# The expert loop of a hybrid decoder step, with the down products moved between the halves of the next expert's gate and up products

## The chip, the cores and the metric

The program runs on one core of a Trainium2 chip. Its time is the device time of one execution in microseconds (us), lower is better; the median of 3 runs of the kernel before is 1805.93 us (1805.49 to 1814.13).

## The reference

One layer of a decoder on 280 tokens (16 meta, 256 prompt, 8 sample tokens), width 2048: norm, a combined input projection, two mixing branches, an output projection; then a mixture of 32 experts, from which each token takes two of one group of eight. Everything is f32. The change touches the experts alone:

```python
p_grp = jax.nn.softmax((xs @ w_coarse + b_coarse).astype(f32), axis=-1)
pg, grp = lax.top_k(p_grp, 1)
...
wt, idx = lax.top_k(jax.nn.softmax(fl_sel, axis=-1), EXPERT_TOP_K)
wt = wt / jnp.sum(wt, axis=-1, keepdims=True) * pg
gate = jnp.zeros((n, N_EXPERTS), f32).at[jnp.arange(n)[:, None], eidx].add(wt)
hg = jnp.einsum('nd,edf->nef', xs, w_gate)
hu = jnp.einsum('nd,edf->nef', xs, w_up)
act = jax.nn.silu(hg) * hu * gate.astype(x.dtype)[:, :, None]
out = jnp.einsum('nef,efd->nd', act, w_down)
```

Per expert w_gate and w_up are 2048 x 512 and w_down is 512 x 2048: three times 4 MiB, 12.58 MB; over 32 experts 402.7 MB.

## The kernel before

The first 740 us or so hold everything ahead of the experts. The routing then makes, on chip, for each expert a rank of its tokens. An expert works on at most 64 tokens (CAP) in a round; further rounds exist for longer lists and are not entered in this input.

**The ring.** All weights pass through `ring`, six slots of 2 MiB. An expert's gate and up weights are cut in two halves along the contracted dimension: the first half sits in slots 2 and 3, the second in 0 and 1 (`MOE_SLOT`). Its down weights are cut in two as well, slots 4 and 5. Each of these six transfers is issued by SyncE (SP), by `load_gate_up` and `load_down`, and waits until PE has used up the slot (`gate_up_done`, `down_done`). Expert 0's six transfers are issued before the loop, while the output projection still runs. In this text a *piece* is a pair of such transfers: first half of gate and up, second half of gate and up, or down.

**An expert x on each engine**, in the kernel before:

- PE (`round_pe`): the list of expert x+1 (`list_of`, 3 small matmuls), gate and up products of x, first and second half (line 1279, 16 matmuls each, which the trace counts as 32), the 16 transposes of the token rows of x+1 (`transpose_rows`, line 1246), the 4 turns of the hidden rows of x (also line 1246), the down products (line 1300, again 16, counted as 32).
- DVE (`round_dve`): the one-hot places for a later list (line 1778), the indices (lines 1783 to 1788), the product h = silu(gate) * up * weight (line 1820), the copy of the turned h (1825), the token rows of x+1 with the gain (1793).
- ACT (`round_act`, unchanged): silu and the copy of up (719, 720), then the four copies of the down results (725).
- GpSimd (`round_rows`): the indirect DMA that scatters the rows of x to `expert_rows` (848), then the gather of the token rows of x+2 (827). These two run on a DMA queue of their own. A gather or scatter has 64 places; places beyond the tokens of the expert are skipped by the bounds check.

PE therefore has, in order, gate/up(x) first half, gate/up(x) second half, down(x), and SP issues loads in the same order, each piece one expert ahead. After the last expert the rows of `expert_rows` are read back, added to x1, normed and stored.

## Time and profile before

| | us |
|---|---|
| median of 3 runs | 1805.93 |
| lowest, highest | 1805.49, 1814.13 |
| the profiled execution | 1807.39 |
| its span, first to last instruction | 1805.5 |
| stage of the experts' loads, first refill issued to last landing | 748.5 to 1747 |

| busy share | PE | PEld | DVE | ACT | POOL |
|---|---|---|---|---|---|
| of the span | 82% | 47% | 33% | 15% | 17% |

The times in the rows below count from the span's start. PE is TensorE's matmuls and PEld its weight loads, DVE VectorE, ACT ScalarE, POOL GpSimd. The share of the DMA engines is a mean over 16 of them. A DMA's time to landing runs from its issue until the last of these engines has delivered its part.

### The profile page before, as it was taken

To read this page: it belongs to the slowest core of one execution; us is meant where nothing else is said; L and a number is where in the kernel's file an instruction comes from. 1 tells how busy PE (TensorE), PEld (TensorE's weight loads), DVE (VectorE), ACT (ScalarE), POOL (GpSimd) and SP (SyncE) were. 2 spreads that over 40 slices of the span, in tenths; PEclk is the share of its full clock that TensorE was granted. 3 is DMA by queue.
4 is the path that set the end of the run, shared out by engine and by line. 5 is a ranking of instruction groups with operands and counts; after the bars stand their busy time and mean duration, and the time that the engine had idled before them with its cause. 6 is when DMAs were issued, how large, how long until landed. Compare 5 with 4: busy or idle time off the path is not lost.

```text
span 1805.5 us, 19311 instructions
## 1 busy us (share of the span) xinstructions
PE 1483.1 (82%) x7485; PEld 853.9 (47%) x7485; DVE 601.2 (33%) x1475; ACT 272.0 (15%) x501; POOL 308.2 (17%) x426
## 2 busy tenths in 40 slices
PE   6999898879988998798878878878877888787780
PEld 6776666567766776443333323323332333233330
DVE  2789999966654113201010100101001010010015
ACT  1100001143331001011111111111111111011111
POOL 0055555443310110000000000000000000000006
PEclk9999899999998999799889889898998989898885
DMA  9433322344513644599999999999999999999954
GB/s 268 141 96 127 105 80 95 107 137 123 171 48 79 221 187 168 215 425 427 420 410 391 408 386 403 418 397 401 396 406 394 405 401 395 397 391 399 393 211 154
DMA packets 130319, 505.28 MB, mean 280 GB/s; under 512 B 23716, under 2 KB 99700, under 8 KB 102780
## 3 DMA queue, kind: packets, MB, share of 16 engines
q1 hardware_dynamic: 112908, 493.74, 70.7%
q0 software_dynamic: 5200, 9.19, 1.6%
q10 hardware_dynamic: 12160, 1.67, 0.7%
q8 instruction: 32, 0.52, 0.1%
q14 instruction: 19, 0.16, 0.0%
HBM read 503.19 MB, written 26.28 MB: 293 GB/s over the span
## 4 chain that ended last, share of the span: by engine, by line
DMA 32%; PE 23%; POOL 2%; issue 1%; DVE 1%; ACT 1%; SPq 1%; POOLq 0%; ACTq 0%; DVEq 0%
DMA ring<-in_w_up_dram 31%; PE bank L1279 17%; PE bank L1300 4%; DVE arena L1820 1%; SPq L383 1%; PE bank L1246 0%; POOL arena L872 0%; POOL arena L871 0%; POOL arena L879 0%; ACT arena L720 0%; POOL arena L880 0%; ACT arena L719 0%; DMA ring<-expert_rows 0%; DVE arena L1825 0%; DMA arena<-x_rows,idx_tok 0%
## 5 line engine op out<-in xcount | busy, mean ns | idle before, releaser
L1279 PE MATMUL bank<-ring,arena 128*64 128x512 f32 x2048 | 486.0, 630 | 97.8 <-DMA ring<-in_w_up_dram 97.8
L1279 PEld LDWEIGHTS bank<-ring,arena 128*64 128x64 f32 x2048 | 196.7, 145 | 360.0 <-issue 359.9
L1300 PE MATMUL bank<-ring,arena 128*64 128x512 f32 x1024 | 277.4, 704 | 18.9 <-DVE arena L1825 18.9
L1820 DVE SCALAR_TENSOR_TENSOR arena<-arena,gcol 64x512 f32<-64x512 f32 x32 | 35.8, 1118 | 635.6 <-ACT arena L720 635.6
L948 PE MATMUL bank<-arena,ring 128*128 128x280 f32 x768 | 195.2, 415 | 0.4 <-DVE arena L1352 0.4
L848 POOL DMA_INDIRECT expert_rows<-arena,idx_dst x32 | 29.4, 920 | 952.1 <-ACT arena L725 952.1
L1300 PEld LDWEIGHTS bank<-ring,arena 128*64 128x64 f32 x1024 | 84.3, 161 | 188.6 <-issue 188.6
L948 PEld LDWEIGHTS bank<-arena,ring 128*128 128x128 f32 x768 | 150.2, 198 | 44.1 <-issue 7.6
L725 ACT ACTIVATE arena<-bank 64x512 f32<-64x512 f32 x128 | 75.7, 592 | 366.7 <-PE bank L1300 365.6
L1246 PE MATMUL bank<-ident,arena 64*128 64x64 f32 x721 | 67.9, 245 | 73.8 <-DVE arena L1820 50.3
L1209 PE MATMUL bank<-ring,arena 128*128 128x256 f32 x512 | 114.6, 386 | 0.0
L1246 PEld LDWEIGHTS bank<-ident,arena 64*128 64x128 f32 x721 | 59.3, 161 | 104.1 <-DVE arena L1820 53.9
L1209 PEld LDWEIGHTS bank<-ring,arena 128*128 128x128 f32 x512 | 98.1, 193 | 16.9 <-issue 3.7
L1783 DVE TENSOR_SCALAR idx_tok<-bank 64x1 uint32<-64x1 f32 x33 | 5.0, 150 | 238.2 <-PE bank L1239 238.2
L1029 PE MATMUL bank<-arena,ring 128*128 128x280 f32 x256 | 75.3, 422 | 0.0
L719 ACT ACT_TABLE_LOAD x16 | 20.5, 1283 | 307.7 <-PE bank L1279 307.7
L940 PE MATMUL bank<-ring,arena 128*128 128x256 f32 x256 | 60.5, 395 | 0.0
L775 POOL TENSOR_TENSOR arena<-arena 128x272 f32<-128x272 f32 x32 | 24.9, 777 | 198.5 <-DVE arena L1538 110.1
L719 ACT ACTIVATE arena<-bank,rcol 64x512 f32<-64x512 f32 x32 | 21.8, 683 | 226.0 <-PE bank L1279 225.8
L940 PEld LDWEIGHTS bank<-ring,arena 128*128 128x128 f32 x256 | 49.9, 198 | 11.0 <-issue 4.2
L1530 DVE TENSOR_TENSOR_SCAN arena<-sc,arena 128x272 f32<-128x272 f32 x64 | 50.0, 820 | 1.1
L1029 PEld LDWEIGHTS bank<-arena,ring 128*128 128x128 f32 x256 | 45.1, 194 | 9.3 <-issue 1.3
(337 smaller groups left out, 1423.9 us busy)
## 6 DMA issues: line engine op xcount, KB each, us to landing
ring<-in_w_down_dram SPq DMA_DIRECT2D x64, 2048.0 KB, 21.2
ring<-in_w_gate_dram SPq DMA_DIRECT2D x64, 2048.0 KB, 18.2
ring<-in_w_up_dram SPq DMA_DIRECT2D x64, 2048.0 KB, 22.9
ring<-in_w_in_dram SPq DMA_DIRECT2D x20, 2048.0 KB, 8.2
ring<-in_w_out_dram SPq DMA_DIRECT2D x8, 2048.0 KB, 9.4
ring<-in_s_w_glu_dram SPq DMA_DIRECT2D x2, 2048.0 KB, 8.4
arena<-v_samples SPq DMA_DIRECT2D x8, 512.0 KB, 4.6
ring<-expert_rows SPq DMA_DIRECT2D x4, 1024.0 KB, 10.2
```

The lines of the kernel that those rows point to most:

```text
L719: nc.scalar.activation(sg[0:CAP, :], PB[b][0:CAP, :], ACT.Silu, scale=rcol[b][:, 0:1])
L725: ins = nc.scalar.activation(yout[b][0:CAP, cc * 512:(cc + 1) * 512], PB[2 + cc // 2][(cc % 2) * CAP:(cc % 2 + 1) * CAP, :], ACT.Copy)
L848: pool.indirect_dma_start(out=y_dram, out_offset=bass.IndirectOffsetOnAxis(ap=idx_dst[b][:, 0:1], axis=0), in_=yout[b][0:CAP, :], in_offse ...
L940: ins = pe.matmul(bank[:, tile * CB:(tile + 1) * CB], xnT[:, k, tile * P:(tile + 1) * P], w[:, k, :], start=(k == 0), stop=(k == KD - 1))
L948: ins = pe.matmul(bank[:, 0:T], w[:, k, b * P:(b + 1) * P], xnT[:, k, :], start=(k == 0), stop=(k == KD - 1))
L1029: ins = pe.matmul(PB[2][:, 0:T], slot(s, KD)[:, k, (i % 2) * P:(i % 2 + 1) * P], xnT[:, k, :], start=(k == 0), stop=(k == KD - 1))
L1209: ins = pe.matmul(PB[unit % 4][:, tile * CB:(tile + 1) * CB], yT[k][:, tile * P:(tile + 1) * P], slot(s, KD)[:, k, :], start=(k == 0), sto ...
L1246: return pe.matmul(out, rows, eye, start=True, stop=True) if waits else pe.transpose(out, rows, eye)
L1279: ins = pe.matmul(PB[b][at:at + CAP, :], xgT[b][:, kk, :], slot(s, KD // 2)[:, k, :], start=(kk == 0), stop=(kk == KD - 1))
L1300: ins = pe.matmul(PB[2 + cc // 2][at:at + CAP, :], hT[:, f, :], slot(4 + half, KF // 2)[:, k, cc * 512:(cc + 1) * 512], start=(f == 0), st ...
L1530: step.add(nc.vector.tensor_tensor_scan(Gs[:, z], sc5[:, 0, j:j + 1].broadcast_to([P, TP]), Wt[:, z], 0.0, ALU.mult, ALU.add))
L1820: STT(hk, sk, gcol[b][:, 0:1], uk, ALU.mult, ALU.mult).then_inc(h_made, 1)
```

## The change

PE's order becomes: list of x+2, gate/up(x) second half, gate/up(x+1) first half, turns of h(x), token rows of x+2, down(x). So silu and the product for x happen while PE has the first half of the next expert, and lists, gathers and transposed rows are made two experts ahead. SP's order follows: gate/up(e+1) first half, down(e), gate/up(e+1) second half. The list's small result has two places in bank 7 now, since its destination and weight columns are read later. GpSimd issues the gather of x+3 first and the scatter of x behind it. The extra, empty list behind the last expert is no longer made: 32 gathers instead of 33.

On PE, one expert in the loop. Of the kernel before (line 1239 the list, 1279 gate and up, 1246 transposes, 1300 down):

```order
463 L1239 MATMUL bank<-route,arena 64x4
464 L1274 ISA
465 L1279 MATMUL bank<-ring,arena 64x512 x16
466 L1274 REGISTER_ALU
467 L1279 MATMUL bank<-ring,arena 64x512 x16
468 L1285 ISA
469 L1246 MATMUL bank<-ident,arena 128x64 x16
470 L1287 REGISTER_ALU
471 L1246 MATMUL bank<-ident,arena 128x64 x4
472 L1292 REGISTER_ALU
473 L1295 REGISTER_ALU
474 L1300 MATMUL bank<-ring,arena 64x512 x16
```

Both halves of one expert stand together, then the 16 token transposes, the 4 turns of h and the down products. The same place in the changed kernel (1250 the list, 1273 gate and up, 1257 transposes, 1292 down):

```order
457 L1250 MATMUL bank<-route,arena 64x4
458 L1268 ISA
459 L1273 MATMUL bank<-ring,arena 64x512 x16
460 L1266 REGISTER_ALU
461 L1268 ISA
462 L1273 MATMUL bank<-ring,arena 64x512 x16
463 L1257 MATMUL bank<-ident,arena 128x64 x4
464 L1310 ISA
465 L1257 MATMUL bank<-ident,arena 128x64 x16
466 L1287 REGISTER_ALU
467 L1292 MATMUL bank<-ring,arena 64x512 x16
```

What moved: the second group at line 1273 belongs to the next expert, and the turns of h stand behind it and ahead of the 16 token transposes.

On SP, the loads of one expert in the loop, with the semaphore that each waits for. Before:

```order
76 L383 ISA [waits gate_up_done]
77 L383 DMA ring<-in_w_gate_dram 128x4096
78 L383 DMA ring<-in_w_up_dram 128x4096 [waits gate_up_done]
79 L383 ISA [waits gate_up_done]
80 L383 DMA ring<-in_w_gate_dram 128x4096
81 L383 DMA ring<-in_w_up_dram 128x4096 [waits gate_up_done]
82 L389 DMA ring<-in_w_down_dram 128x4096 [waits down_done] x2
```

In the changed kernel, in the loop over e:

```order
80 L383 ISA [waits gate_up_done]
81 L383 DMA ring<-in_w_gate_dram 128x4096
82 L383 DMA ring<-in_w_up_dram 128x4096 [waits gate_up_done]
83 L494 ISA
84 L389 ISA [waits down_done]
85 L389 DMA ring<-in_w_down_dram 128x4096
86 L389 ISA [waits down_done]
87 L389 DMA ring<-in_w_down_dram 128x4096
88 L383 ISA [waits gate_up_done]
89 L383 DMA ring<-in_w_gate_dram 128x4096
90 L383 DMA ring<-in_w_up_dram 128x4096 [waits gate_up_done]
```

The two down transfers stand between the two halves of the next expert; the number and size of transfers are the same.

```diff
@@ SP
             def round_loads(R):
-                with sp.Fori(1 if is_first(R) else 0, NE) as e:
+                def gate_up_half(e, half):
                     x = e + R * NE
-                    for q in range(4):
-                        sp.wait_ge(gate_up_done, x * 2 + (q // 2 - 1))
+                    for q in (2 * half, 2 * half + 1):
+                        sp.wait_ge(gate_up_done, x * 2 + (half - 1))
                         load_gate_up(e, q)
...
+                gate_up_half(1, 0)
...
+                gate_up_half(1, 1)
+                with sp.Fori(1, NE - 1) as e:
+                    gate_up_half(e + 1, 0)
+                    down(e)
+                    gate_up_half(e + 1, 1)
+                down(NE - 1)
@@ GpSimd
+            def rows_of_pair(R, i, gathers):
                 for b in range(2):
                     x = i * 2 + (R * NE + b)
-                    g = i * 2 + (R * (NE + 1) + b + 1)
-                    pool.wait_ge(tr_done, g)
-                    gather(g, 1 - b)
...
+                    if b < gathers:
+                        pool.wait_ge(tr_done, x + 3)
+                        gather(x + 3, 1 - b)
                     pool.wait_ge(rows_ready, x + 2)
...
+                    pool.wait_ge(scattered[b], i * 16 + (R * (NE // 2) + 1) * 16)
+                    pool.sem_inc(rows_free, 1)
@@ PE
+            def pair_pe(R, i, last):
+                for b in range(2):
+                    x = i * 2 + (R * NE + b)
+                    if not last:
+                        pe.wait_ge(dst_ready, x + 1)
+                        list_of(x + 2, i * 2 + (b + 2), b)
+                    gate_up(x, b, 1)
+                    if not (last and b):
+                        gate_up(x + 1, 1 - b, 0)
+                    turn_h(x)
+                    if not last:
+                        pe.wait_ge(gathered[b], i * 16 + (R * (NE // 2) + 2) * 16)
+                        transpose_rows(b)
+                    down(x)
...
+                for e in range(2):
+                    list_of(R * NE + e, e, e)
...
+                transpose_rows(0)
+                gate_up(R * NE, 0, 0)
...
+                transpose_rows(1)
@@ DVE
+            def pair_dve(R, i, lists, turns):
+                for b in range(2):
+                    x = i * 2 + (R * NE + b)
+                    if turns:
+                        tokens(x + 2, b)
+                    dve.wait_ge(act_ready, x + 1)
...
+                    STT(hk, sk, gcol[b][:, 0:1], uk, ALU.mult, ALU.mult).then_inc(h_made, 1)
+                    dve.wait_ge(hT_done, x + 1)
...
+                    if turns:
+                        columns(b)
+                        rows_in(x + 2, b)
+                    if turns or b == 0:
+                        destinations(x + 1, 1 - b)
+                    if b < lists:
+                        places(i * 2 + (b + 3))
```

## Rows read from the trace of the kernel before

**Rows 1.** The page's 40 slices of the span, 45 us each

```profile
PE   6999898879988998798878878878877888787780
...
PEclk9999899999998999799889889898998989898885
DMA  9433322344513644599999999999999999999954
GB/s 268 141 96 127 105 80 95 107 137 123 171 48 79 221 187 168 215 425 427 420 410 391 408 386 403 418 397 401 396 406 394 405 401 395 397 391 399 393 211 154
```

**Rows 2.** Groups by line, 748.5 to 1747: xcount, busy us, mean ns, idle before

```profile
L1279 PE MATMUL bank<-ring,arena 128*64 128x512 f32 x2016 | 477.3, 628 | 97.8 <-DMA ring<-in_w_up_dram 97.8
L1300 PE MATMUL bank<-ring,arena 128*64 128x512 f32 x992 | 267.4, 701 | 18.3 <-DVE arena L1825 18.3
...
L1246 PE MATMUL bank<-ident,arena 64*128 64x64 f32 x704 | 65.6, 243 | 69.3 <-DVE arena L1820 50.3 <-DMA arena<-x_rows,idx_tok 19.0
```

**Rows 3.** Windows, whole stage: length, busy us by engine, PEclk, DMA share, GB/s

```profile
748.50:1747.00 998.50, 812.99 (x3898) 344.09 (x3894) 105.20 (x282) 134.72 (x204) 57.54 (x62) 0.90 0.98 400
```

**Rows 4.** Chain that ended last, 1200 to 1300: start us, us, what

```profile
1192.46 28.39 DMA ring<-in_w_up_dram
...
1220.98 8.71 PE bank L1279 x32
...
1230.27 19.84 DMA ring<-in_w_up_dram
...
1250.24 7.10 PE bank L1279 x32
...
1257.92 26.70 DMA ring<-in_w_up_dram
...
1294.58 19.85 DMA ring<-in_w_up_dram
```

**Rows 5.** DMA issues between 1215.7 and 1216.5: count, KB, us to landing

```profile
ring<-in_w_gate_dram SPq DMA_DIRECT2D x1, 2048.0 KB, 19.9
ring<-in_w_up_dram SPq DMA_DIRECT2D x1, 2048.0 KB, 24.4
```

**Rows 6.** Windows, 1220 to 1235

```profile
1220.00:1225.00 5.00, 4.02 (x12) 1.43 (x14) 0.00 (x0) 0.00 (x0) 0.00 (x0) 0.57 1.00 426
...
1227.50:1230.00 2.50, 2.50 (x16) 0.87 (x12) 0.00 (x0) 0.21 (x1) 0.00 (x0) 1.00 0.52 223
1230.00:1232.50 2.50, 1.19 (x18) 1.05 (x17) 1.18 (x2) 1.07 (x2) 0.00 (x0) 1.00 0.86 288
```

**Rows 7.** Line 383, gate and up loads, issued 756 to 1740

```profile
DMA to landing us min/median/max: 10.5/19.9/28.4
```

**Rows 8.** Line 389, down loads, issued 756 to 1740

```profile
DMA to landing us min/median/max: 11.0/21.4/26.4
```

**Rows 9.** Line 383, two loads issued one at a time, 670 to 700

```profile
DMA to landing us min/median/max: 7.2/7.3/7.3
```

**Rows 10.** Last load of the stage, issued between 1727 and 1729

```profile
ring<-in_w_down_dram SPq DMA_DIRECT2D x1, 2048.0 KB, 19.3
```

**Rows 11.** Timeline, first experts: start us, us, engine, line, idle before

```profile
730.32 0.15 DVE L1783 TENSOR_SCALAR idx_tok<-bank 64x1 uint32<-64x1 f32 x1 [0.96 <-PE bank L1239]
...
731.54 1.15 POOL L827 DMA_INDIRECT arena<-x_rows,idx_tok  x1 [17.42 <-DVE gcol L1785]
...
737.09 1.29 DVE L1793 TENSOR_TENSOR arena<-bank,gain_ffn 128x512 f32<-128x512 f32 x2 [6.42 <-PE bank L1246]
...
739.32 1.11 PE L1279 MATMUL bank<-ring,arena 128*64 128x512 f32 x1
...
748.46 0.35 SPq L383 DMA_DIRECT2D ring<-in_w_gate_dram  x1
```

**Rows 12.** Timeline, end of an expert's down products, 1242 to 1247

```profile
1242.32 2.40 ACT L725 ACTIVATE arena<-bank 64x512 f32<-64x512 f32 x4 [11.24 <-PE bank L1300]
...
1242.60 0.15 DVE L1783 TENSOR_SCALAR idx_tok<-bank 64x1 uint32<-64x1 f32 x1 [7.78 <-PE bank L1239]
...
1245.54 0.92 POOL L848 DMA_INDIRECT expert_rows<-arena,idx_dst  x1 [34.39 <-ACT arena L725]
...
1246.77 0.94 POOL L827 DMA_INDIRECT arena<-x_rows,idx_tok  x1 [0.30 <-issue]
```

**Rows 13.** Timeline, last expert

```profile
1724.23 3.77 SPq L389 DMA_DIRECT2D ring<-in_w_down_dram  x2
...
1736.46 7.09 PE L1279 MATMUL bank<-ring,arena 128*64 128x512 f32 x32 [1.63 <-DMA ring<-in_w_up_dram]
...
1747.49 9.97 PE L1300 MATMUL bank<-ring,arena 128*64 128x512 f32 x32 [0.59 <-DVE arena L1825]
```

More of the change, by code:

```diff
@@ L1251, in transpose_rows, with gate_up @@
                 ins.then_inc(tr_done, 1)
+            def gate_up(x, b, half):
+                if half == 0:
+                    pe.wait_ge(xgT_ready, x + 1)
+                sg_, su_ = MOE_SLOT[2 * half], MOE_SLOT[2 * half + 1]
+                pe.wait_ge(slot_loaded[sg_], x * 16 + 16 * (FILLS[sg_] + 1))
+                pe.wait_ge(slot_loaded[su_], x * 16 + 16 * (FILLS[su_] + 1))
+                for k in range(KD // 2):
+                    kk = half * (KD // 2) + k
+                    for at, s in ((0, sg_), (CAP, su_)):
+                        ins = pe.matmul(PB[b][at:at + CAP, :], xgT[b][:, kk, :], slot(s, KD // 2)[:, k, :],
+                                        start=(kk == 0), stop=(kk == KD - 1))
+                ins.then_inc(gate_up_done, 1)
@@ new lines, in turn_h, with down @@
+            def turn_h(x):
+                pe.wait_ge(h_made, x + 2)
+                for f in range(KF):
+                    ins = turn_64(PB[6][:, f * CAP:(f + 1) * CAP], hh[0:CAP, f * P:(f + 1) * P], f == 0)
+                ins.then_inc(hT_done, 1)
+            def down(x):
+                pe.wait_ge(hT_ready, x + 1)
+                pe.wait_ge(rows_ready, x + 1)
+                for half in range(2):
+                    pe.wait_ge(slot_loaded[4 + half], x * 16 + 16)
+                    for k in range(KF // 2):
+                        f = half * (KF // 2) + k
+                        for cc in range(4):
+                            at = (cc % 2) * CAP
+                            ins = pe.matmul(PB[2 + cc // 2][at:at + CAP, :], hT[:, f, :],
+                                            slot(4 + half, KF // 2)[:, k, cc * 512:(cc + 1) * 512],
+                                            start=(f == 0), stop=(f == KF - 1))
+                    ins.then_inc(down_done, 1)
@@ L1305, in _ @@
+                pair_pe(R, NE // 2 - 1, True)
             run_rounds(pe, round_pe)
@@ L1828, in _ @@
+                destinations(x0, 0)
+                for e in range(2):
+                    rows_in(x0 + e, e)
+                with dve.Fori(0, NE // 2 - 2) as i:
+                    pair_dve(R, i, 2, True)
+                pair_dve(R, NE // 2 - 2, 1, True)
+                pair_dve(R, NE // 2 - 1, 0, False)
             run_rounds(dve, round_dve)
```

127 lines of the change are left out of this document (40 added, 87 removed).

## The prediction

> **What bounds the kernel now.** I read the 40 slices first. From slice 18 to slice 38 the DMA row stands at 9 and the rate at about 400 GB/s, while PE drops to 7 and 8 [rows 1]. That is the expert stage, and only it is touched. Then I read the groups by line in it: PE waits 97.8 us for the up weights, 50.3 for the product h, 18.3 for the copy of the turned h, 19.0 for gathered rows [rows 2]. PE is busy 813 of 998.5 us, the DMA engines 0.98 [rows 3]. So the stage looks bound by loads, but not quite full, and the question that decides is whether the missing 2% is something a new order can get back.
>
> The chain answers it. Four second-half up loads, one per expert, land at 1192.46 + 28.39 = 1220.85, then 1250.11, 1284.62 and 1314.43 [rows 4]. Six transfers of 2 MiB land in each gap: 29.26, 34.51 and 29.81 us. The shortest gap is 4.88 us a transfer, 12.58 MB in 29.26 us or 430 GB/s, which is the rate of a full window too (426) [rows 6]. So in that gap the engine that lands last never paused. Yet inside the same gap, from 1227.5 to 1232.5, the mean share falls to 0.52 and 0.86 and the rate to 223 and 288 GB/s [rows 6]. Both hold at once only if the 16 engines aren't level: at 1227.5 the loads issued at 1215.4 and 1215.8 are still 8 and 12.7 us from landing (19.9 and 24.4 us after issue [rows 5]), so some engine has two or more transfers ahead of it while about half have nothing. A load counts as landed when the last engine has it. The dips are idle time of the early engines. The late one sets the pace.
>
> Is the late one ever empty? A load that meets no other takes 7.2 us [rows 9]: 4.88 of transfer and 2.3 of start. In the stage none took under 10.5 us, and the median is 19.9 and 21.4 [rows 7, 8]. Every load was thus issued at least 3.2 us, mostly some 12 us, before the late engine could begin it. Freeing a slot earlier lengthens that queue and brings nothing forward.
>
> The stage adds up on that reading. First refill issued at 748.46 [rows 11]; last load issued at 1727.7 (second of the pair that starts at 1724.23 [rows 13]), landing 19.3 us later [rows 10], at 1747.0: 998.5 us. It has 31 x 6 = 186 transfers: 7.3 for the first, 185 x 4.88 = 902.8, and 88.4 left. In each expert there is one scatter and one gather, so a pair of them costs the late engine 88.4 / 31 = 2.85 us. (The chain agrees: the 34.51 us gap is 5.2 longer than 29.26 and takes in two pairs.)
>
> At this place a rule of the Trainium skill speaks against the change. DMA: Bandwidth & Descriptors, section Latency and other measured facts, says that DMA engines 7 and 15 are usually slower, by its best guess since descriptors of GpSimd's transfers are fetched through their ports. The trace agrees as far as it can: some engines fall behind here, but which ones they are, and whether they are always the same, no row tells. By that rule the gain is nil, as in the sum below.
>
> **The change part by part.**
>
> *Silu and h behind the next expert's first half.* PE's waits for h and its copy, 50.3 + 18.3 us [rows 2], go, and so should most of the 19.0 for gathered rows. PE's own work stays (477.3 + 267.4 + 65.6 us, about 26 of 32.2 us an expert). What is late next is the same thing as now, the late engine: PE reaches each piece earlier and waits there. Worth 0 in the sum. If this cover were gone, i.e. if PE set the pace, the 69 us would be the gain.
>
> *The order of the loads.* Same 186 transfers, same slots; each is again issued when PE has used up the piece three pieces back. A piece is used up at most 9.97 us after it lands (slow case of 32 matmuls [rows 13]), and at that time two pieces, 4 x 4.88 = 19.5 us, are still to come. 19.5 - 10.0 - 2.3 = 7.2 us in hand. Cost 0.
>
> *Gather ahead of scatter.* Now the scatter is issued at 1245.54 and the gather at 1246.77 [rows 12]. In the new order the gather waits for the indices alone, 1.2 us after they start (730.32 to 731.54 [rows 11]), so at about 1243.8; the scatter still waits for ACT's copies, which end at 1244.7, so about 1245.5. They stand 1.7 us apart rather than 1.2, in the other order, with the same 64 places each. Both queue behind the same weight traffic. I take the price of a pair as unchanged. Its bounds: from 0 (-88 us over the stage) to, with nothing shared between the two any more, twice 2.85 (+88); the row nearest to it is today's pair, so the middle, and I keep half a microsecond a pair either way, 15 us, in mind for the range. POOL's queue has a longer wait in it: the gather of x+3 behind the landing of the scatter before. That one was issued an expert, 32 us, earlier. Nothing is held up.
>
> *One gather fewer.* The empty one behind the last expert goes. It moves no rows; between 0 and 2.85 us, I take -0.4.
>
> *The start.* The list of expert 1 comes before the rows of expert 0 are there, so the first product can start when DVE's gain ends at 737.09 + 1.29 = 738.4 instead of 739.32 [rows 11]: -0.8. Behind the first half PE now does 16 transposes and a list before the second (1.8 us), and then the first half of expert 1 before its next refill is issued. By durations of the rows: first piece refilled at 747.6, landing at 754.9 and 759.8; second half done and refilled at about 757, landing by 769.5; first half of expert 1 from 759.8, 7.1 to 8.7 us, so its refill goes out at 767 to 768.6 and its data can flow 2.3 later, 769.3 to 770.9. The queue could run dry for 0 to 1.4 us, once. I take +0.5.
>
> *The end.* Last lands down(31), as now; before it the second half of expert 31, as now at 1736.3. But PE has then been idle since down(30), which landed two transfers earlier (1726.5) and takes some 4.4 us more: about 5 us idle instead of 1.63. After an idle of 5.77 us PE's clock is granted at 0.57 on average over 5 us (1.2 GHz for most of it [rows 6]) and 32 matmuls take 8.71 us instead of 7.10 [rows 4]: +1.6, in the path, since the down products of the last expert follow. Bounds 0 to 2.9 (7.10 to 9.97).
>
> Sum: 1807.39 - 0.4 - 0.8 + 0.5 + 1.6 = 1808.3 for a profiled execution. The profiled one stood 1.46 above its median of 1805.93, so 1806.8 for the median.
>
> **The rivals.**
>
> *The dips are refilled (faster).* If the late engine isn't a fixed few, or its lag comes from late refills, then earlier and more even refills give the idle share back. For it: the rate falls under 400 GB/s in slice after slice [rows 1], and the rate in them is half. Trace Analysis, section Optimization Strategy, of the Trainium skill says that consistent bubbles can mean too little room for the next tile, which would here be slots freed late; this trace has the bubbles, but the loads behind them were already issued. Against it: the shortest landing of 10.5 us, and 29.26 us for six transfers right across a dip. Gain: by share 2% of 998.5, 20 us; by rate 998.5 x (1 - 400/428) = 65 us, which takes in the pairs' real cost. Middle 42: 1765 us.
>
> *The indirect pair gets dearer (slower).* One mechanism: gather and scatter, 1.2 us apart now, share what they cost the late engine; issued in the other order and further apart, they pay more apiece. It decides from 0.3 us a pair on (31 x 0.3 = 9 us). For it: pairs cost 2.85 us though they move few bytes, so the price is one of handling, not of volume. Against it: both still lie in the air together. At +0.8 us a pair 25 us: 1832 us.
>
> *The change doesn't do what it says:* PE's wait for h stays since PE reaches the turns before ACT and DVE are through. They need about 4 us, the half in between 7.1. And the time would be the same.
>
> **How the numbers follow.** No change that matters 0.70 (its own range 1799 to 1815: start and end, and a fifth of a microsecond a pair); dips refilled 0.17 (1742 to 1787); dearer pairs 0.13 (1817 to 1850). 0.5% is 9 us, about what can be told from no change here. Faster: 0.17 + 0.04 of the first case's edge = 0.21. Slower: 0.13 + 0.05 = 0.18. Same: 0.61. Range 1780 to 1824: it leaves out about 0.13 below and 0.07 above.
>
> **What would show it.** Right: the last load lands about 998 us after the first refill; no line's shortest landing comes under about 9 us past the start; six transfers between two second-half up loads still take 29.3 us or more; PE's waits for line 1820's successor are gone and its waits for ring loads have grown by about as much, now on down weights too. The dips stay, perhaps smaller. Wrong: a stage under 980 us with the rate above 410 GB/s (dips refilled), or over 1010 us with loads landing as slowly as now (dearer pairs), or landings near 7.2 us in mid-stage (the queue runs dry).

## The result, and the profile after

The changed kernel takes 1794.98 us (median of 5 runs, 1794.28 to 1797.34), the kernel before 1808.01 (5 runs, 1805.49 to 1814.13): ratio 0.993, 95% interval 0.991 to 0.9949. That is 0.7% faster. The forecast was 1806.8 us and no change. The time lies in the range of 1780 to 1824 that was given, but below the 1799 to 1815 of the case that had 0.70 of the chances.

The profiled execution took 1796.58 us, 10.8 less than before. Its page, in the same 40 slices as [rows 1]:

```profile
PE   6999889879988999697878778788877878878770
...
PEclk9999999889998999698989999898998899889985
DMA  9423323334522753599999999999999999999944
GB/s 270 141 94 99 122 84 97 115 102 126 173 81 62 219 208 137 217 392 424 422 418 403 404 419 402 386 418 405 407 402 407 400 408 413 408 407 403 414 198 155
```

The picture is the old one: 9 in the DMA row from slice 18 on, and PE at 7 and 8. Only the rate is a little higher, 404 GB/s over the stage instead of 400. PE's groups by line in the stage (count, busy us, mean ns, idle before and its releaser) are to be compared with [rows 2]:

```profile
L1273 PE MATMUL bank<-ring,arena 128*64 128x512 f32 x2016 | 522.5, 678 | 183.3 <-DMA ring<-in_w_up_dram 183.3
L1292 PE MATMUL bank<-ring,arena 128*64 128x512 f32 x992 | 219.7, 596 | 0.5 <-DVE arena L1838 0.5
L1257 PE MATMUL bank<-ident,arena 64*128 64x64 f32 x682 | 55.3, 234 | 0.0
```

The waits for h, its copy and the gathered rows, 50.3 + 18.3 + 19.0 us, are gone but for 0.5 us. The one wait left to speak of is for the up weights: 183.3 us instead of 97.8, or 85.5 more for the 87.6 that went. That exchange bought nothing. The whole stage, from first refill to last landing, is to be compared with [rows 3]; the last two columns are DMA share and GB/s:

```profile
747.10:1733.90 986.80, 801.53 (x3870) 319.63 (x3870) 105.32 (x274) 134.70 (x204) 56.52 (x61) 0.91 0.99 404
```

986.8 us instead of 998.5 carries the gain: the stage starts 1.3 us earlier (747.12 for 748.46), is 11.7 shorter, and what follows its last landing is 2.2 longer (60.7 for 58.5): -10.8 in all.

The chain of waits, four landings of second-half up loads as in [rows 4] (start, us):

```profile
1194.57 22.43 DMA ring<-in_w_up_dram
...
1227.80 20.77 DMA ring<-in_w_up_dram
...
1258.94 21.85 DMA ring<-in_w_up_dram
...
1290.32 21.55 DMA ring<-in_w_up_dram
```

They land at 1217.00, 1248.57, 1280.79 and 1311.87: gaps of 31.57, 32.22 and 31.08 us, none under 29.3. From 771 us on no gate or up load took under 11.9 us to land and no down load under 13.3, so each was still issued well before the last engine could begin it. What lies in each gap beside six transfers is GpSimd's pair, here from the timeline (start, us), against [rows 12]:

```profile
1246.22 0.93 POOL L843 DMA_INDIRECT arena<-x_rows,idx_tok  x1 [28.65 <-DVE idx_tok L1810]
1248.22 0.92 POOL L857 DMA_INDIRECT expert_rows<-arena,idx_dst  x1 [1.07 <-ACT arena L741]
```

The gather now stands 2.0 us ahead of the scatter, where it stood 1.2 us behind it. For the transfers issued between 760 and 1730 us, issue to landing takes this long, first the gathers, then the scatters:

```profile
DMA to landing us min/median/max: 7.9/9.0/11.0
...
DMA to landing us min/median/max: 8.2/10.1/12.1
```

The same of the kernel before, gathers and scatters:

```profile
DMA to landing us min/median/max: 10.1/11.6/14.1
...
DMA to landing us min/median/max: 7.6/8.6/10.7
```

In both kernels the one that stands behind takes longer to land, but the pair as a whole shrank: 1.2 + 11.6 = 12.8 us from first issue to last landing, now 2.0 + 10.1 = 12.1.

By the prediction's own formula, (stage - 7.3 - 902.8) / 31, a pair cost the late engine 2.85 us before and 2.47 now. 2.6 us of the new stage are a dry queue at the start (below), and without them it is 2.39. By this reckoning 31 x 0.46 = 14.3 us is what the pairs gave back, and 14.3 - 2.6 = 11.7. It closes by construction, since the pairs get all that is left over; whether it is they that changed is for the runs to show.

### The profile page after: what moved, and what is told of

Same layout as the page of the kernel before. It is cut to its first block, busy times and chain, and to the rows that moved or that the text cites. A ratio compares the mean times of both kernels' runs of the same rounds, so it can differ in the third digit from the quotient of the medians.

```text
span 1794.6 us, 19292 instructions
## 1 busy us (share of the span) xinstructions
PE 1472.8 (82%) x7462; PEld 828.1 (46%) x7462; DVE 602.2 (34%) x1468; ACT 271.9 (15%) x501; POOL 305.8 (17%) x425
## 4 chain that ended last, share of the span: by engine, by line
DMA 40%; PE 25%; DVE 1%; POOL 1%; issue 1%; SPq 1%; ACT 0%; POOLq 0%; ACTq 0%; DVEq 0%
DMA ring<-in_w_up_dram 39%; PE bank L1273 15%; PE bank L1220 6%; PE bank L1292 1%; PE bank L929 1%; SPq L383 1%; DMA ring<-expert_rows 0%; PE bank L1187 0%; PE bank L1170 0%; POOL arena L890 0%; PE bank L1198 0%; POOL arena L891 0%; PE bank L1257 0%; PE bank L1240 0%; DVE arena L1877 0%
## 5 line engine op out<-in xcount | busy, mean ns | idle before, releaser
L1273 PE MATMUL bank<-ring,arena 128*64 128x512 f32 x2048 | 531.4, 678 | 184.7 <-DMA ring<-in_w_up_dram 183.3
L1273 PEld LDWEIGHTS bank<-ring,arena 128*64 128x64 f32 x2048 | 188.2, 155 | 503.2 <-issue 501.6
L843 POOL DMA_INDIRECT arena<-x_rows,idx_tok x32 | 30.1, 942 | 862.3 <-DVE idx_tok L1810 862.0
L1292 PEld LDWEIGHTS bank<-ring,arena 128*64 128x64 f32 x1024 | 71.3, 138 | 133.4 <-issue 130.0
L1838 DVE COPY arena<-bank 128x256 f32<-128x256 f32 x32 | 13.6, 424 | 315.6 <-PE bank L1257 315.6
L1220 PEld LDWEIGHTS bank<-ring,arena 128*128 128x128 f32 x512 | 97.8, 192 | 16.8 <-issue 3.7
L1257 PEld LDWEIGHTS bank<-ident,arena 64*128 64x128 f32 x704 | 53.8, 156 | 32.4 <-issue 26.0
L1257 PE MATMUL bank<-ident,arena 64*128 64x64 f32 x704 | 58.6, 237 | 5.5 <-DMA arena<-x_rows,idx_tok 2.9
L1823 DVE TENSOR_TENSOR arena<-bank,gain_ffn 128x512 f32<-128x512 f32 x64 | 41.2, 686 | 33.3 <-PE bank L1257 33.3
## 6 DMA issues: line engine op xcount, KB each, us to landing
ring<-in_w_up_dram SPq DMA_DIRECT2D x64, 2048.0 KB, 22.2
```

The source lines that it names most:

```text
L843: pool.indirect_dma_start(out=xg[p][0:CAP, :], out_offset=None, in_=x1_dram, in_offset=bass.IndirectOffsetOnAxis(ap=idx_tok[p][:, 0:1], ax ...
L1220: ins = pe.matmul(PB[unit % 4][:, tile * CB:(tile + 1) * CB], yT[k][:, tile * P:(tile + 1) * P], slot(s, KD)[:, k, :], start=(k == 0), sto ...
L1257: return pe.matmul(out, rows, eye, start=True, stop=True) if waits else pe.transpose(out, rows, eye)
L1273: ins = pe.matmul(PB[b][at:at + CAP, :], xgT[b][:, kk, :], slot(s, KD // 2)[:, k, :], start=(kk == 0), stop=(kk == KD - 1))
L1292: ins = pe.matmul(PB[2 + cc // 2][at:at + CAP, :], hT[:, f, :], slot(4 + half, KF // 2)[:, k, cc * 512:(cc + 1) * 512], start=(f == 0), st ...
L1823: ins = TTo(xgT[p][:, 8 * q:8 * q + 8, :], PB[4 + q][:, :].rearrange("p (a n) -> p a n", a=8), gain_ffn[:, 8 * q:8 * q + 8].unsqueeze(2).b ...
```

## The experiments

In all of them the stage is the time from the first refill's issue to the last landing, and "price" is (stage - 910.1) / 31, that of a pair with whatever the start leaves dry (0 to 4 us, up to 0.14 a pair). Ratios are against the kernel before, run beside each kernel on the same chip (medians of 1805.5 to 1808).

Stage and price come from one profiled execution each, the time from 4 to 10. The profiled one often stood 2 to 3 us from its kernel's median, in run 14 5.1 below it and in run 3 6.5 below. 3 us are 0.1 us in the price, so prices that differ by 0.1 or less are not told apart. Some expectations speak of 2.3 us a pair (3.5 in run 11), from another reckoning; the table's figures for the same kernels are 2.47 and 3.72.

| | edit | us | ratio, 95% | stage | price |
|---|---|---|---|---|---|
| before | | 1808.0 | | 998.5 | 2.85 |
| after | | 1795.0 | 0.9929, 0.991-0.9949 | 986.8 | 2.47 |
| 1 | before, gather first | 1795.3 | 0.9938, 0.9918-0.9957 | 986.0 | 2.45 |
| 2 | after, scatter first | 1801.3 | 0.9965, 0.9951-0.9979 | 995.1 | 2.74 |
| 3 | after, gather behind the scatter's landing | 1817.1 | 1.0048, 1.0029-1.0068 | 1003.9 | 3.03 |
| 4 | after, gather first, 1.2 us apart | 1796.8 | 0.9944, 0.9927-0.996 | 986.6 | 2.47 |
| 5 | one empty gather more | 1800.5 | 0.9967, 0.9955-0.9979 | 989.3 | 2.55 |
| 6 | 32 places | 1795.5 | 0.9936, 0.9916-0.9956 | 981.3 | 2.30 |
| 7 | scatter 16 places | 1792.8 | 0.9917, 0.989-0.9944 | 976.5 | 2.14 |
| 8 | gather 16 places | 1786.1 | 0.988, 0.9857-0.9903 | 977.2 | 2.16 |
| 9 | after, tokens spread | 1793.3 | 0.9929, 0.9901-0.9957 | 986.5 | 2.46 |
| 10 | before, spread | 1799.2 | 0.9959, 0.9945-0.9974 | 991.5 | 2.63 |
| 11 | after, places packed | 1835.2 | 1.015, 1.0126-1.0175 | 1025.3 | 3.72 |
| 12 | before, gather first, spread | 1795.7 | 0.9925, 0.99-0.9949 | 988.8 | 2.54 |
| 13 | after, odd experts in partitions 64 on | 1798.3 | 0.9954, 0.9937-0.997 | 988.7 | 2.54 |
| 14 | 13, spread | 1796.5 | 0.9938, 0.9915-0.9962 | 987.6 | 2.50 |
| 15 | no rows gathered | 1743.7 | 0.9652, 0.9626-0.9678 | 937.9 | 0.90 |
| 16 | no rows scattered | 1781.6 | 0.9861, 0.9834-0.9889 | 966.5 | 1.82 |
| 17 | rows selected on TensorE | 1749.6 | 0.9691, 0.9675-0.9707 | 940.0 | 0.96 |
| 18 | 2, no rows scattered | 1784.8 | 0.9893, 0.987-0.9916 | 970.7 | 1.95 |

### Which part of the change does it: 1 to 4

**1.** The kernel before, with GpSimd's order alone changed. PE, DVE, ACT and SP keep their order. As in the changed kernel, GpSimd waits for each scatter's landing right behind it.

```diff
-                    pool.wait_ge(tr_done, g)
-                    gather(g, 1 - b)
...
+                    if b < gathers:
+
+                        pool.wait_ge(tr_done, g)
+                        gather(g, b)
                     pool.wait_ge(rows_ready, x + 2)
...
+                    pool.wait_ge(scattered[b], i * 16 + (R * (NE // 2) + 1) * 16)
+                    pool.sem_inc(rows_free, 1)
```

> The kernel before with GpSimd's order of the change alone: the gather for the expert after next is issued first, the scatter some 2 us behind it, PE's and SP's orders as before. Theory A (the saving of some 13 us is the price of the indirect pair on the late DMA engine, 2.85 to 2.39 us): most of it comes back here, 1794 to 1799 us. Theory B (the saving comes from the order of the loads and of PE's work): no gain, 1805 to 1810 us.

1795.33 us: all of the change's gain. The stage of this kernel, and PE's wait between 750 and 1680 us:

```profile
747.60:1733.60 986.00, 808.05 (x3898) 346.94 (x3894) 105.09 (x282) 134.71 (x204) 57.49 (x62) 0.91 0.99 405
```

```profile
L1242 PE MATMUL bank<-ident,arena 64*128 64x64 f32 x660 | 61.5, 240 | 58.6 <-DVE arena L1816 58.6
```

PE still waits 58.6 us for h, in a stage as short as the changed kernel's. With the gather first, the new order of products and loads adds nothing.

**2.** The changed kernel with the scatter first again, the gather 1.2 us behind it.

```diff
-                        gather(x + 3, 1 - b)
                     pool.wait_ge(rows_ready, x + 2)
...
+                        gather(x + 3, 1 - b)
```

> The changed kernel with the scatter issued first and the gather right behind it, 1.2 us later, as before the change; PE and SP unchanged. Theory A: the gain is gone, 1806 to 1811 us (the two or three us lost at start and end come on top of the old price). Theory B: 1794 to 1797 us, as the changed kernel.

1801.33 us, between both theories: about half of the gain goes. The stage gets 8.3 us back, and gathers land after 11.5 us in the median again. So the order counts in this kernel too. But with the scatter first the new order of products and loads keeps 5.5 us over the kernel before (ratio 0.9965, clear of noise), 0.1 to 0.2 us a pair. Where that rest comes from wasn't found.

**3.** The gather waits until the scatter of the same turn has landed.

```diff
-                    if b < gathers:
-
-                        pool.wait_ge(tr_done, x + 3)
-                        gather(x + 3, 1 - b)
...
                     pool.wait_ge(scattered[b], i * 16 + (R * (NE // 2) + 1) * 16)
                     pool.sem_inc(rows_free, 1)
+                    if b < gathers:
+
+                        pool.wait_ge(tr_done, x + 3)
+                        gather(x + 3, 1 - b)
```

> The changed kernel with each gather issued only when the scatter before it has landed, so that the two never overlap. If the price falls with the distance between the two: below the changed kernel, down to 1785 us. If only the order (gather ahead) counts: 1804 to 1811. If two apart cost as much as twice one: above 1810. Theory B: 1794 to 1797, since PE and SP are unchanged.

1817.1 us, 1.2% above the changed kernel. PE's group for the transposes says that this isn't a clean measure of the pair:

```profile
L1257 PE MATMUL bank<-ident,arena 64*128 64x64 f32 x687 | 89.0, 305 | 195.1 <-DMA arena<-x_rows,idx_tok 192.5 <-DVE arena L1836 2.6
```

PE stands 192.5 us for gathered rows, so its refills may be late too. The run only says that keeping the two apart in time is no cure.

**4.** Gather first, held back until the scatter can go too.

```diff
                     x = i * 2 + (R * NE + b)
+                    pool.wait_ge(rows_ready, x + 2)
                     if b < gathers:
```

> The changed kernel with the gather held until the rows to scatter are ready: gather first, scatter 1.2 us behind it instead of 2.0. If the order alone counts: 1794 to 1797 us. If the distance alone counts: 1804 to 1811 us. Theory B: 1794 to 1797 us.

1796.79 us and a price of 2.47 (its profiled execution was 2.9 us faster than its median), with 1.2 us between the two as in run 2. 4.5 us lie between the two runs and 1.8 between this one and the changed kernel: it is mainly the order, and not the distance or the earlier time of issue.

### What the price is made of: 5 to 8, 15, 16

**5.** One gather more per expert, all of its 64 places skipped.

```diff
+                    pool.indirect_dma_start(out=no_rows[:, :], out_offset=None, in_=t["w_coarse"][0],
+                                            in_offset=bass.IndirectOffsetOnAxis(ap=idx_none[:, 0:1], axis=0),
+                                            bounds_check=last_none, oob_is_err=False).then_inc(none_done, 16)
```

> The changed kernel with one more indirect gather per expert between gather and scatter, whose 64 places are all skipped: no row moves. If the price of an indirect transfer on the late DMA engine is that of handling its places, a third transfer costs about 1 us an expert: 1820 to 1830 us. If it is that of the rows moved: 1795 to 1798 us. One in which nothing moves but the order still counts would lie between.

The time rises by some 5 us, 0.17 us an expert, and the price by 0.08: above the 1795 to 1798 expected if rows alone set the price, far under the 1820 to 1830 of places. An indirect transfer that moves nothing is cheap.

**6, 7, 8.** Fewer places: 32 in both, 16 in the scatter, 16 in the gather. Rows beyond them are left out. Kernels whose scatter leaves rows out fill `expert_rows` once beforehand (runs 6, 7, 16 and 18), which delays the first refill to between 752 and 756 us, 5 to 9 later than in the changed kernel. Of these runs the stage is to be compared and not the time.

```diff
-                pool.indirect_dma_start(out=xg[p][0:CAP, :], out_offset=None, in_=x1_dram,
+                pool.indirect_dma_start(out=xg[p][0:32, :], out_offset=None, in_=x1_dram,
...
-                                            in_=yout[b][0:CAP, :], in_offset=None, bounds_check=last_row,
+                                            in_=yout[b][0:32, :], in_offset=None, bounds_check=last_row,
```

```diff
-                                            in_=yout[b][0:CAP, :], in_offset=None, bounds_check=last_row,
+                                            in_=yout[b][0:16, :], in_offset=None, bounds_check=last_row,
```

```diff
-                pool.indirect_dma_start(out=xg[p][0:CAP, :], out_offset=None, in_=x1_dram,
+                pool.indirect_dma_start(out=xg[p][0:16, :], out_offset=None, in_=x1_dram,
```

> The changed kernel with 32 instead of 64 places in each gather and scatter: tokens beyond the 32nd of an expert are left out, and the buffer of the expert rows is filled once ahead of the loop. Most lists are shorter than 32, so most rows still move. If the places set the price: the pair falls from about 2.3 to some 1.3 us, 1763 to 1775 us. If the rows set it: 1788 to 1796 us.

> The changed kernel with 16 places in each scatter and 64 in each gather (tokens beyond the 16th of an expert are not stored; the buffer of the expert rows is filled once ahead of the loop). If the two transfers share one price: the saving is under a quarter of a pair's, 1787 to 1796 us. If each pays for itself by its places: three quarters of half the pair's price, some 27 us off, 1765 to 1773 us.

> The changed kernel with 16 places in each gather and 64 in each scatter (tokens beyond the 16th of an expert get no rows of their own). By the same two readings: 1787 to 1796 us if the pair shares one price, 1765 to 1773 us if each pays by its places. If e7 and this one differ by more than 8 us, one of the two transfers carries the price.

The queue of the indirect transfers (packets, MB, share of 16 engines over the span), from the pages of the changed kernel and of run 6:

```profile
q0 software_dynamic: 5120, 9.19, 1.6%
```

```profile
q0 software_dynamic: 3072, 8.84, 1.5%
```

Run 6 drops half of the places (40% of the packets) and 4% of the bytes and saves 0.17 us a pair; runs 7 and 8 drop 14% of the bytes and save about 0.32. Places count for little, rows for much.

**15, 16.** All places skipped, in the gathers (so no expert gets its token rows), and in the scatters (no routed row is added).

```diff
-                                        in_offset=bass.IndirectOffsetOnAxis(ap=idx_tok[p][:, 0:1], axis=0),
+                                        in_offset=bass.IndirectOffsetOnAxis(ap=idx_none[:, 0:1], axis=0),
```

```diff
-                    pool.indirect_dma_start(out=y_dram, out_offset=bass.IndirectOffsetOnAxis(ap=idx_dst[b][:, 0:1], axis=0),
+                    pool.indirect_dma_start(out=y_dram, out_offset=bass.IndirectOffsetOnAxis(ap=idx_none[:, 0:1], axis=0),
```

> The changed kernel with every place of the gathers skipped: 64 places are handled, no row is read, the experts work on rows left from before. Scatters as ever. If scatter and gather behind each other share their time on the late engine, the scatter alone costs nearly the whole price of the pair: 1780 to 1795 us. If each pays its own, about half of 2.3 us an expert is saved: 1755 to 1768 us.

> The changed kernel with every place of the scatters skipped, so that no expert row is stored (the buffer is filled once ahead of the loop, which puts some 8 us ahead of the stage in e6 and e7). By the same two readings: shared price 1785 to 1798 us, each its own 1758 to 1775 us.

The slices of run 15, and its q0 row:

```profile
GB/s 277 146 97 97 97 97 97 97 122 124 173 113 23 238 179 160 140 352 428 427 428 427 428 428 428 427 428 427 421 427 427 423 427 418 426 416 423 421 203 159
...
q0 software_dynamic: 5120, 4.61, 0.8%
```

1743.7 us is below both expectations, the lower of which was 1755 to 1768, and 1781.6 lies between its two. So the two transfers don't share one price, and the gather's is by far the larger. Without gathered rows the stage runs at 427 or 428 GB/s in its first ten full slices and at 416 to 427 behind them. (The Trainium skill, HBM Reference, section Specifications (TRN2), puts a core that streams alone at about 425 GB/s, bound by its 16 DMA engines; this trace agrees, with 427 and 428.) Gathered rows cost 2.47 - 0.90 = 1.57 us an expert, scattered rows 2.47 - 1.82 = 0.65, and the rest, 0.2 to 0.3, is places, issue and start. Yet the gathers' packets took only 1.6 - 0.8 = 0.8% of the span on the mean engine, 14 us, while the stage lost 31 x 1.57 = 49. A gather costs the stage more than three times what its packets take on the mean engine.

Where the rest goes can be read from the packets. While the rows of a gather move, the DMA engines are busy and yet slow. Of run 16 (gathers only) two such stretches, and one of run 15 in which the rows of a scatter move; the last two columns are DMA share and GB/s:

```profile
1311.00:1313.50 2.50, 2.50 (x12) 1.02 (x10) 0.00 (x0) 0.00 (x0) 0.00 (x0) 0.77 1.11 298
1495.00:1498.00 3.00, 3.00 (x14) 1.01 (x12) 0.00 (x0) 0.00 (x0) 0.00 (x0) 0.75 1.04 298
```

```profile
1223.50:1227.00 3.50, 3.50 (x16) 1.30 (x14) 0.00 (x0) 0.00 (x0) 0.00 (x0) 0.82 1.02 431
```

Twelve stretches of run 16 have 262 to 410 GB/s, twelve of run 15 417 to 462. The weights move in 23808 packets of 16 KB, half of which take 608 to 613 ns; 8 of 611 ns in a row are the 4.88 us of a transfer. That gives three parts of what the mean engine spends beyond its weights at full rate. They are summed over the packet records of the traces, in us over the stage:

| | rows' own packets | weight packets, beyond 611 ns each | idle |
|---|---|---|---|
| before | 28.3 | 43.1 | 16.1 |
| after | 27.4 | 33.8 | 14.6 |
| 1, before, gather first | 26.8 | 36.8 | 11.5 |
| 2, after, scatter first | 27.4 | 39.4 | 17.3 |
| 11, places packed | 26.5 | 39.1 | 48.7 |
| 15, no rows gathered | 12.9 | 11.6 | 2.4 |
| 16, no rows scattered | 17.1 | 32.4 | 6.0 |

Of the 49 us that gathered rows cost ("after" less run 15), 14.5 are their own packets, 22.2 slower weight packets and 12.2 idle time. Only the last part, beside a dry queue at the start, is time in which the mean engine waits for the late one. The slower weight packets come with gathered rows: in run 16, 919 of the 1254 weight packets that start while such rows move take over 700 ns, and in run 15, with scattered rows, 9 of 1446. Why reading rows slows the weights beside them, no run here shows.

**18.** Run 2 without scattered rows: is it those rows, ahead of the gather, that make scatter first dearer?

```diff
-                    pool.indirect_dma_start(out=y_dram, out_offset=bass.IndirectOffsetOnAxis(ap=idx_dst[b][:, 0:1], axis=0),
+                    pool.indirect_dma_start(out=y_dram, out_offset=bass.IndirectOffsetOnAxis(ap=idx_none[:, 0:1], axis=0),
```

> The changed kernel with GpSimd's scatter issued 1.2 us ahead of the gather (as in the run with scatter first), and all 64 places of each scatter marked as skipped, so that the routed rows are not added to the output. With the gather first the same omission gave 1781.6 us (13 us under the changed kernel), and scatter first with its rows cost 1801.3. Theory A (the surcharge of scatter first is an interplay of the scattered rows with the gathered ones behind them): without scattered rows the order costs nothing, about 1782. Theory B (the gather itself is dearer when it is issued later beside the weight loads): the surcharge stays, 1801 less 13, about 1788 or more.

1784.82 us, midway, and the price differs from run 16's by 0.13 where 2 differs from the changed kernel by 0.27. The 95% interval, 1782.0 to 1790.3 us by the ratio, takes in both theories (1782 and 1788). Inconclusive.

### Which engine gets which row: 9 to 14

If the late engine is late because several rows of a pair fall to it, then other places for the tokens should move the price. The list puts the n-th token in place n; here it goes to every fourth place in turn (runs 9, 10, 12, 14), or into as few groups of places as can be (run 11).

```diff
-            nc.vector.tensor_copy(slotid, iota_i[:, 0:CAP])
+            nc.vector.tensor_copy(slotid.rearrange("p (a b) -> p a b", b=4), iota_i[:, 0:CAP].rearrange("p (b a) -> p a b", b=4))
```

```diff
-            nc.vector.tensor_copy(slotid, iota_i[:, 0:CAP])
+            nc.vector.tensor_copy(slotid.rearrange("p (h c q) -> p h c q", h=2, q=4),
+                                  iota_i[:, 0:CAP].rearrange("p (c h q) -> p h c q", h=2, q=4))
```

> The changed kernel with an expert's tokens spread over the 64 places: the token of rank r takes place 4 (r mod 16) + r div 16 instead of place r, so that some 17 rows touch partitions 0, 4, 8 ... 60 and not 0 to 16. Theory C (the late DMA engines are those whose share of the places is filled first: with four neighbouring places or partitions to an engine or a port, the first 16 tokens load four of them with four rows each): the price of the pair falls from 2.3 to about 1 us, 1750 to 1770 us. If the price has nothing to do with places: 1793 to 1798 us. If places go round the engines one by one, spreading by four puts four rows on every fourth engine: above 1810 us.

> The kernel before with the same spreading of tokens over places and nothing else. Theory C: 1755 to 1785 us; how far it stays above e9 shows what the change's order of PE's work and loads is worth once the late engines are relieved. If the price has nothing to do with places: 1804 to 1810 us.

> The kernel before with the gather issued ahead of the scatter (as in e1) and the tokens spread (as in e9). If e9 and this one agree within 3 us, the order of PE's work and of the loads is worth nothing even then; if e9 is lower by 5 us or more, it is worth that much once the late engines are relieved. Theory C puts it at 1750 to 1775 us.

> The changed kernel with the tokens packed the other way: ranks 0 to 3 at places 0 to 3, 4 to 7 at places 32 to 35, 8 to 11 at 4 to 7, and so on, so that eight rows fall on one group of eight partitions {4c .. 4c+3, 32+4c .. 32+4c+3}, which the Trainium skill (SBUF - State Buffer, The DMA port swizzle) says share one DMA port. If the port decides: the price rises towards twice, 1830 to 1865 us. If four neighbouring places on one engine decide: 1793 to 1799 us, as the changed kernel.

Spread changes nothing that can be told where the gather is first (2.46 against 2.47, 2.54 against 2.45), so the 1750 to 1770 us of theory C fell. It takes 0.22 us off where the scatter is first (2.63 against 2.85, 1799.2 us). Packed, the price rises to 3.72 and the time by 2.2% over the changed kernel's. By the table above this is idle time of the mean engine, 48.7 us for 14.6: here the engines are less level. The slices of run 11:

```profile
DMA  9434222343515454699999999999999999999954
GB/s 266 137 99 132 92 92 93 99 146 119 164 38 148 147 230 166 246 427 426 399 375 391 401 376 392 386 392 393 383 388 405 373 396 371 396 399 375 394 228 151
```

So the place of a row does matter, in one direction: rows packed into few groups of places are dear. (SBUF — State Buffer, section Door 1: The DMA port swizzle, of the Trainium skill groups partitions 0 to 3 with 32 to 35 on one port, and so on; run 11 fills these groups one after the other, and its price fits that.) By the same map partitions 64 to 127 have ports of their own:

```diff
-                pool.indirect_dma_start(out=xg[p][0:CAP, :], out_offset=None, in_=x1_dram,
+                pool.indirect_dma_start(out=xg[p][p * CAP:(p + 1) * CAP, :], out_offset=None, in_=x1_dram,
...
-                                            in_=yout[b][0:CAP, :], in_offset=None, bounds_check=last_row,
+                                            in_=yout[b][b * CAP:(b + 1) * CAP, :], in_offset=None, bounds_check=last_row,
```

> The changed kernel with the token rows and result rows of every second expert in partitions 64 to 127 instead of 0 to 63 (gather, transposes, result copies and scatter alike). Theory C, now by ports (e11 raised the price of a pair from 2.3 to 3.5 us by putting eight rows on a port): the rows of neighbouring experts load different ports and so different late engines, an engine pays in every second expert only, and the ring evens that out: 1755 to 1775 us. If the late engines are late for another reason than the partitions that rows go to: 1793 to 1798 us.

> As e13, and the tokens spread over the 64 places as in e9. Theory C: not above e13, 1750 to 1772 us; by e9 the spreading alone is worth 0 to 2 us. Otherwise 1793 to 1798 us.

2.54 and 2.50: no gain from the other half of the partitions (the transposes read there too), with or without spread. The gather for x+3 and the scatter of x stand in different halves here, so the price isn't that two transfers meet at a port. Whether the rows of one transfer in run 11 meet at a port, or at an engine chosen by the place in the list, these runs don't tell apart.

### A kernel that beats both: 17

Only experts 0 and 1 still gather. For the other 30, TensorE selects the token rows from x1, which is in SBUF anyway, by the one-hot matrix of the places, and ScalarE copies them out (of the edit, the matmuls are shown).

```diff
+            def select_rows(g):
+                pe.wait_ge(xgT_ready, g)
+                for tile in range(3):
+                    n = TT[tile]
+                    for cc in range(4):
+                        at = (cc % 2) * CAP
+                        ins = pe.matmul(PB[4 + cc // 2][at:at + CAP, :], oh[0:n, tile, :], x1[0:n, tile, cc * 512:(cc + 1) * 512],
+                                        start=(tile == 0), stop=(tile == 2))
+                ins.then_inc(sel_done, 1)
```

> The changed kernel without its gathers from HBM for experts 2 to 31: TensorE selects the 64 rows of an expert from x1 in SBUF by the one-hot matrix of its places (12 matmuls an expert into two banks), ScalarE copies them out, and the transposes follow as before; 30 of 32 gathers of 64 rows go, the scatters stay. Theory (the late DMA engine bounds the stage, and a gather costs it about 1.6 us an expert, as the run without gathered rows showed with 1743.7 us): 30 x 1.6 = 48 us less than the changed kernel's 1795, about 1745 to 1755, if TensorE still waits for weights. Rival (TensorE becomes the bound): it works about 25 us an expert in a period of 30.8 and gets some 5 us more in the same period that would shrink to 29.2; then its waits for up loads are gone from the trace and the time is 1765 to 1800.

1749.64 us (1747.59 to 1750.08), 3.1% under the kernel before, with all of the computation in it. Its slices, its stage, and PE's groups:

```profile
PE   6999988979998999699999999999999999999870
...
PEclk9999999989999999699999999999999999999985
...
GB/s 277 146 97 97 96 97 97 97 121 124 173 112 23 236 179 162 142 312 426 428 428 428 429 428 428 428 429 428 424 419 430 424 429 420 428 419 430 422 207 159
```

```profile
747.00:1687.00 940.00, 890.62 (x4590) 346.14 (x4590) 107.00 (x275) 278.73 (x337) 27.73 (x31) 0.99 0.99 420
```

```profile
L1283 PE MATMUL bank<-ring,arena 128*64 128x512 f32 x2016 | 452.5, 603 | 46.0 <-DMA ring<-in_w_up_dram 46.0
...
L1313 PE MATMUL bank<-arena 128*64 128x512 f32 x720 | 167.9, 598 | 0.9 <-DVE arena L1844 0.9
```

720 matmuls of 598 ns are 168 us more work, 5.6 an expert, and they cost 6 us over run 15, which gathers nothing at all. They fall in PE's waits, now 46.0 us instead of 183.3. With PE pausing less, its clock is granted at 0.99 instead of 0.91, so line 1283's matmuls take 603 ns where line 1273's took 678 and give 70 us back. The stage is at the loads' limit: (940.0 - 910.1) / 31 = 0.96 us is left of the price.

## Why the prediction failed, step by step

- **What bounds.** Held: the loads set the stage, and the one engine that lands last is never empty but at the start. Each weight load's 16 parts land one by one: in the medians of the six slots 13 come within 4 us of the first, and the last 8.5 to 11.3 us behind it before, 9.5 to 10.7 after. But the lag itself is the small part. The mean engine is idle for 16.1 us of the stage, and most of the 88 us that the prediction laid on the late engine is paid by all: 28.3 for the rows' packets and 43.1 for slower weight packets. With the gather first PE's order is worth nothing: run 1 has the old order and the new time.
- **"Worth 0 in the sum" for silu and h.** Held, to 2 us: 87.6 us of waits went, 85.5 came back behind the up loads.
- **"The order of the loads. Cost 0."** Held in mid-stage: none of the gaps in the chain is under 29.3 us. SP's order and PE's make no gain beside gather first (run 1), and a part of one, 0.1 to 0.2 us a pair, beside scatter first (run 2), for which I have no cause.
- **"Gather ahead of scatter ... I take the price of a pair as unchanged."** This is the step that failed. It fell from 2.85 to 2.39 us, 14.3 us over 31 pairs, and run 1 shows that GpSimd's order alone gives the whole gain. The half microsecond kept either way for the range just covers it, and that is why the range held though the forecast failed. But the 0 in the sum was the middle between two far bounds, and not worked out from anything about the order. One sign was at hand: the gather in second place took 11.6 us to land and the scatter in first place 8.6, so the two might not be alike. The runs then showed that they are not: a gather's rows are worth 1.57 us an expert and a scatter's 0.65, and nothing made the sum the same after an exchange.
- **"One gather fewer", -0.4.** Not to be told apart; an empty gather costs 0.08 to 0.17 us (run 5).
- **The start**, -0.8 and +0.5 with a dry queue of 0 to 1.4 us. The stage started 1.3 us earlier, and the queue ran dry for 2.6. The last load of the second piece, issued at 756.15, landed 14.1 us later, at 770.2. The next went out at 770.27 and landed at 777.7: 7.5 us behind the one before it, 2.6 more than the 4.88 of a transfer. Timelines of PE and of SP (start, us):

```profile
760.32 9.78 PE L1273 MATMUL bank<-ring,arena 128*64 128x512 f32 x32 [4.59 <-DMA ring<-in_w_up_dram]
```

```profile
756.15 0.43 SPq L383 DMA_DIRECT2D ring<-in_w_up_dram  x1
770.27 0.35 SPq L383 DMA_DIRECT2D ring<-in_w_gate_dram  x1
```

The first half of expert 1 took 9.78 us, not 7.1 to 8.7, since PE had waited 4.59 us ahead of it and its clock had fallen: 0.72 was granted from 760.3 to 770.1. The term is off by 2.1.
- **The end**, +1.6 for a slower second half of expert 31:

```profile
1722.53 9.95 PE L1273 MATMUL bank<-ring,arena 128*64 128x512 f32 x32 [4.31 <-DMA ring<-in_w_up_dram]
```

9.95 instead of 7.09, the far end of the bounds given; what follows the last landing is 2.2 longer.
- **The rivals.** "Dips refilled" asked for a stage under 980 us and over 410 GB/s: neither. "Dearer pairs" named the right resource and the wrong sign; its reason, a price "of handling, not of volume", is wrong too, since skipped places cost little and rows much (runs 5, 15, 16). "The change doesn't do what it says" fell: PE's waits for h are 0.5 us.
- **The signs.** The stage is 986.8 us, not about 998. The shortest landings (11.9 and 13.3 us) and the gaps are as foretold. PE's waits grew by as much as went, but none of them on down weights.

By the terms: 1807.4 - 1.3 (start) + 2.6 (dry) - 14.3 (pairs, what is left over) + 2.2 (end) = 1796.6.

Open is why a gather is cheaper ahead of a scatter than behind it. It is the order, not the distance (run 4), and not places (run 5). Where the time is saved can be seen: the rows' own packets take about the same (28.3 and 27.4 us), while the weight packets' excess falls from 43.1 to 33.8, 9.3 of the 11.7 us by which the stage shrank (to 36.8 in run 1, where idle time falls by 4.6 as well; back to 39.4 in run 2). Why the weights suffer less is not shown. Run 18 says that about half of it goes with the scattered rows, within an error as large.

## What to carry to other kernels

Where a stage is bound by loads, ask what small transfers cost the stage in all, and not what their own packets take: beside those they can slow the packets of the loads and set the engines apart. Here 35 rows an expert take 7 to 9% of the stage where their packets take under 3%, and none of PE's waits names them. The order in which two such transfers are issued is part of the work and wants a bound with a sign of its own. The better cure is to take the rows from what SBUF holds already, in PE's idle time: 168 us of added matmuls cost some 6 us, and kept the clock up.

## What the hardware showed that I had not expected

- Gathered rows cost 2.4 times as much as scattered ones of the same bytes, 1.57 against 0.65 us an expert, beside full weight streams. While they move, most of the weight packets that start take over 700 ns instead of 611 (run 16); beside scattered rows hardly any do (run 15).
- Packing rows into few groups of places made the pair 1.25 us dearer (run 11), while moving them to the other half of the partitions did nothing (run 13).
- With all 64 places of its gathers skipped the kernel moves 421 GB/s over the stage (run 15), and with its rows 404.
